# Both output projections of a two-layer hybrid decoder by seven products over pairs of token tiles

## What is computed

```python
def _cross_attn(x, mem_k, mem_v, wq, wo):
    q = (x @ wq).reshape(B, T, XA_HEADS, XA_HEAD_DIM)
    s = jnp.einsum('bthd,bnhd->bhtn', q, mem_k).astype(F32) * XA_HEAD_DIM ** -0.5
    p = jax.nn.softmax(s, axis=-1).astype(x.dtype)
    o = jnp.einsum('bhtn,bnhd->bthd', p, mem_v).reshape(B, T, -1)
    return o @ wo

def _layer(x, pos, mem_k, mem_v, state, P):
    ...
    mix = jnp.concatenate([y_m, y_r, y_g, y_w], axis=-1).astype(x.dtype) @ P['w_out']
    x = _layer_norm(ALPHA * x + mix, P['ln1_g'], P['ln1_b'])
    x = _layer_norm(ALPHA * x + _cross_attn(x, mem_k, mem_v, P['xa_wq'], P['xa_wo']), P['ln2_g'], P['ln2_b'])
    ff = jnp.square(jax.nn.relu(x @ P['w_up'])) @ P['w_down']
    x = _layer_norm(ALPHA * x + ff, P['ln3_g'], P['ln3_b'])
```

## Time and profile before

| | |
|---|---|
| Time, median of 3 runs (range) | 2280.8 us (2274.9 to 2288.0) |
| Profiled execution, span from first to last instruction | 2275.9 us |
| PE busy | 2222.5 us, 98% |
| DVE busy | 1096.5 us, 48% |
| ACT busy | 431.2 us, 19% |
| POOL busy | 115.4 us, 5% |
| Granted TensorE clock, mean | 0.994 |

### The profile page before, as it was taken

The page is one execution under the profiler, slowest core; times in us unless marked ns, Lnnn a source line. Parts: engine busy times, 40 slices in busy tenths (PEclk is TensorE's granted clock), DMA queues, the critical chain, the costliest instruction groups (busy, mean ns, idle before and its releaser), DMA issues. The chain is left out here.

```text
span 2275.9 us, 32156 instructions
## 1 busy us (share of the span) xinstructions
PE 2222.5 (98%) x13494; PEld 1626.9 (71%) x13494; DVE 1096.5 (48%) x1951; ACT 431.2 (19%) x915; POOL 115.4 (5%) x208
## 2 busy tenths in 40 slices
PE   7999999999999999999999999999999999999997
PEld 5877765547855888888888777565488468888885
DVE  5652246545425444765166422655354364447643
ACT  2332122021311222000023321311114012120000
POOL 0111101000100000000002111010000000000000
PEclk9999999999999999999999999998999999999998
DMA  7121114234442122222142112233346222222221
GB/s 282 55 72 40 50 47 122 86 105 185 185 148 93 53 96 74 74 74 90 58 132 75 38 40 58 55 109 109 114 151 223 107 93 74 74 94 92 75 74 39
DMA packets 136335, 217.27 MB, mean 95 GB/s; under 512 B 33672, under 2 KB 67776, under 8 KB 136064
## 3 DMA queue, kind: packets, MB, share of 16 engines
q1 hardware_dynamic: 133888, 211.02, 27.1%
q10 hardware_dynamic: 2304, 4.20, 0.5%
HBM read 198.39 MB, written 14.58 MB: 94 GB/s over the span
## 5 line engine op out<-in xcount | busy, mean ns | idle before, releaser
L727 PE MATMUL psum<-xT,ring 128*128 128x256 f32 (+1 forms) x768 | 222.1, 415 | 0.1
L2270 PE MATMUL psum<-tmp 128*128 128x272 f32 x768 | 181.4, 393 | 0.1
L2270 PEld LDWEIGHTS psum<-tmp 128*128 128x128 f32 x768 | 145.8, 190 | 30.8 <-issue 0.9
L727 PEld LDWEIGHTS psum<-xT,ring 128*128 128x128 f32 x768 | 131.3, 189 | 35.2 <-issue 10.2
L724 PE MATMUL psum<-ring,ext 128*128 128x512 f32 x256 | 126.0, 629 | 0.0
L677 PE MATMUL psum<-xT,ring 128*128 128x256 f32 (+1 forms) x512 | 120.3, 394 | 4.4 <-ACT big L1817 2.0
L2371 PE MATMUL psum<-big,ring 128*128 128x256 f32 (+1 forms) x512 | 118.4, 393 | 0.0
L677 PEld LDWEIGHTS psum<-xT,ring 128*128 128x128 f32 x512 | 96.3, 190 | 25.7 <-issue 4.6
L2689 PE MATMUL psum<-ring,big 128*128 128x512 f32 x256 | 113.1, 595 | 0.0
L827 PE MATMUL psum<-ring,big 128*128 128x512 f32 x256 | 111.9, 594 | 0.0
L2371 PEld LDWEIGHTS psum<-big,ring 128*128 128x128 f32 x512 | 97.0, 190 | 19.8
(11 more groups left out here) (494 smaller groups left out, 3553.8 us busy)
## 6 DMA issues: line engine op xcount, KB each, us to landing
ring<-in_w_down SPq DMA_DIRECT2D x16, 2048.0 KB, 7.7
ring<-in_w_in SPq DMA_DIRECT2D x14, 2048.0 KB, 8.6
ring<-in_w_up SPq DMA_DIRECT2D x14, 2048.0 KB, 7.7
big<-in_cache_mem_k SPq DMA_DIRECT2D x16, 1024.0 KB, 6.9
ring<-in_xa_wk SPq DMA_DIRECT2D x4, 2048.0 KB, 8.7
ring<-in_xa_wv SPq DMA_DIRECT2D x4, 2048.0 KB, 10.3
ring<-in_w_out SPq DMA_DIRECT2D x4, 2048.0 KB, 9.1
ring<-in_xa_wq SPq DMA_DIRECT2D x4, 2048.0 KB, 7.9
```

Of the source, the lines that this page charges most:

```text
L727: ins = pe.matmul(bank[:, :c.stop - c.start], wring[:, n % 2, k, i * P:(i + 1) * P], xTv[:, k, c], start=(k == 0), stop=(k == KC - 1))
L2270: ins = pe.matmul(ps[:, :HT], left[:, k, :], right[:, k, :], start=(k == 0), stop=(k == KH - 1))
```

## The change

Each of the two output projections is computed for pairs of token tiles, (0, 1) and (2, 3). With input halves by depth (first and last four chunks of 128) and output halves of 512 columns, a pair takes seven products of four chunks (numbered 1 to 7) where it took eight. Products 1, 2, 4 and 5 start a bank; 6 is piled on 1's bank, 3 on 5's, 7 on 6's, each after DVE has read what is there. The sums of weights are made on POOL, the sums of inputs on DVE. `residual` is called 18 times in a projection where it was called 10 times; eight of the 18 are a plain addition. Transposed x has its columns in a new order (`PLACE`): tiles 0, 1, the samples, 2, 3, in the layers' two normed x that feed the query and the MLP.

```diff
+PLACE = [0, P, 2 * P + NS, 3 * P + NS, 2 * P]
+TOKEN_PAIRS = ((0, 1), (2, 3))
...
+            def pair_product(pe, pre, p, i, bank, left, right):
+
+                ps = bk.begin(pe, (pre, p, i), bank)
+                for k in range(4):
+                    ins = pe.matmul(ps, left(k), right[:, k, :], start=(k == 0 and i in (1, 2, 4, 5)), stop=(k == 3), skip_group_check=True)
+                bk.filled(ins, (pre, p, i))
...
             def wout_ahead(pe):
 
-                for half in range(2):
-                    slab_wait(pe, 11 + half)
+                slab_wait(pe, 11)
                 pe.wait_ge(sig["yC"], sig.at("yC", 1))
                 pe.wait_ge(sig["yD"], sig.at("yD", 1))
-                for T in range(2):
-                    wout_tile(pe, T, range(4, KC))
+                for p in range(2):
+                    wout_product(pe, p, 2, p)
+                pe.wait_ge(sig["wright"], sig.at("wright", 3))
+                for p in range(2):
+                    wout_product(pe, p, 4, 2 + p)
+
+            def wout_weights(g):
+
+                bk.take(g, ("Bsc", 4))
+                slab_wait(g, 11)
+                slab_wait(g, 12)
+                w0, w1 = wring[:, 1], wring[:, 0]
+                t1, t2, t4 = wout_right
+                after(g, g.tensor_tensor(t1, w1[:, 0:4], w0[:, 0:4], ALU.subtract), "wright")
+                after(g, g.tensor_tensor(t2, w1[:, 4:8], t1, ALU.subtract), "wright")
+                after(g, g.tensor_tensor(t4, w0[:, 4:8], t2, ALU.subtract), "wright")
...
+                    wout_sums(v)
                     ps = bk.take(v, ("orow2",))
...
-                    turn_x_tensor(pe, bk, sig, LN1, 3, 4, (4, 5))
+                    turn_x_tensor(pe, bk, sig, LN1, 2, 3, (4, 5))
                     for u in range(4):
                         if u == 0:
                             q_first(2)
-                            for T in (4, 3):
+                            turn_x_tensor(pe, bk, sig, LN1, 3, 4, (4, 5))
+                            for T in (2, 3):
...
+                    def left_sums(p, which):
+
+                        ta, tb = (slice(TILES[T][0], TILES[T][0] + P) for T in TOKEN_PAIRS[p])
+                        for hp in range(2):
+                            bk.given(v, ("pv", TOKEN_PAIRS[p][1], hp))
+                        for j in which:
+                            if j in (1, 2):
+                                v.wait_ge(sig["aleft"], sig.at("aleft", 4 * p + j))
+                            a, b_, op = ((aT[:, 0:4, tb], aT[:, 4:8, tb], ALU.add), (left_a[0], aT[:, 0:4, ta], ALU.subtract),
+                                         (aT[:, 4:8, ta], left_a[1], ALU.subtract), (aT[:, 0:4, ta], aT[:, 0:4, tb], ALU.subtract))[j]
+                            sig.up(v.tensor_tensor(left_a[j], a, b_, op), "aleft")
...
                         if T < 3:
                             maxima(T + 1)
+                        if T == 2:
+                            left_sums(0, range(4))
...
                     for hp in range(2):
                         bk.take(g, ("s", 3, hp))
                     after(g, g.memset(pOwn, 0.0), "pOwn0")
+                    slab_wait(g, 15)
+                    slab_wait(g, 16)
+                    w0, w1 = wring[:, 1], wring[:, 0]
+                    after(g, g.tensor_tensor(right_a[0], w1[:, 0:4], w0[:, 0:4], ALU.subtract), "aright")
+                    after(g, g.tensor_tensor(right_a[1], w1[:, 4:8], right_a[0], ALU.subtract), "aright")
+                    bk.take(g, ("ss",))
+                    after(g, g.tensor_tensor(right_a[2], w0[:, 4:8], right_a[1], ALU.subtract), "aright")
```

More of the change, by code:

```diff
@@ new lines, in wout_last_weights, with wout_sums @@
+            def wout_last_weights(g):
+                bk.take(g, ("wout", "part", 1))
+                w1 = wring[:, 0]
+                after(g, g.tensor_tensor(w1[:, 0:4], w1[:, 4:8], w1[:, 0:4], ALU.subtract), "wright")
+            def wout_sums(v):
+                for n in "ABCD":
+                    v.wait_ge(sig["y" + n], sig.at("y" + n, 1))
+                tiles = [[slice(TILES[T][0], TILES[T][0] + P) for T in pair] for pair in TOKEN_PAIRS]
+                for p in range(2):
+                    tb = tiles[p][1]
+                    ins = v.tensor_tensor(quartered(wout_left[p][0]), y_low[:, :, :, tb], y_high[:, :, :, tb], ALU.add)
+                    sig.up(ins, "wleft")
+                for p in range(2):
+                    ta, tb = tiles[p]
+                    s1, s2, s4, s3 = (quartered(s_) for s_ in wout_left[p])
+                    if p == 0:
+                        v.wait_ge(sig["wleft"], sig.at("wleft", 2))
+                    sig.up(v.tensor_tensor(s2, s1, y_low[:, :, :, ta], ALU.subtract), "wleft")
+                    sig.up(v.tensor_tensor(s3, y_low[:, :, :, ta], y_low[:, :, :, tb], ALU.subtract), "wleft")
+                    v.wait_ge(sig["wleft"], sig.at("wleft", 3 * p + 3))
+                    sig.up(v.tensor_tensor(s4, y_high[:, :, :, ta], s2, ALU.subtract), "wleft")
@@ L834, in wout_ahead, with sample_fold, wout_tensor @@
+            def sample_fold(pe, pre, banks):
+                for half in range(2):
+                    bk.given(pe, (pre, "part", half))
+                    ps = bk.begin(pe, (pre, 4, half), banks[half])
+                    bk.filled(pe.matmul(ps[:NS, :], const("fold"), partial[:, half, :], start=True, stop=True), (pre, 4, half))
+            def wout_tensor(pe):
                 for half in range(2):
                     slab_wait(pe, 11 + half)
-                pe.wait_ge(sig["yC"], sig.at("yC", 1))
@@ L2224, in residual @@
                 ps = bk.take(v, key)
-                bk.give(v.scalar_tensor_tensor(x, x, ALPHA, ps[:n, :], ALU.mult, ALU.add), key)
-                bk.given(v, key)
+                if more:
+                    ins = v.tensor_tensor(x, x, ps[:n, :], ALU.add)
+                else:
+                    ins = v.scalar_tensor_tensor(x, x, ALPHA, ps[:n, :], ALU.mult, ALU.add)
+                if done:
+                    bk.give(ins, key)
+                    bk.given(v, key)
+                else:
+                    v.wait_ge(sig["v"], sig.up(ins, "v"))
             hT = cols(big, 0, FC, NT)
```

273 lines of the change are left out of this document (160 added, 113 removed).

## The result

The change makes the kernel slower: 2301.6 us median (2299.5 to 2306.9) against 2280.5 in the same runs, a ratio of 1.0104 with a 95% interval of 1.0077 to 1.0132. (The ratio is the record's estimate over the runs of both kernels; the two medians alone lie 21.1 us apart, 1.0093, inside the interval.) I had forecast 2290, within 0.5% of before, and a range of 2272 to 2302, whose upper end the time just meets. The profiled execution spans 2298.8 us, 22.9 more than before's.

A forecast was written before the change was run, and what follows sets the result against it. PE, busy 2222.5 of 2275.9 us, was taken to bound the kernel. Terms of +1.7 a layer, +3.4 in two, gave a 2279.3 span; 4.9 to the median made 2284.2, and the clock's 6.0 made 2290, range 2272 to 2302.

The forecast's parts named there:

- Saved products: Both output projections: 112 records of 128 by 512 instead of 128, -7.0 us each, -28.0 for four.
- The block's end: End of the first block: POOL's three weight sums and DVE's work alternate, next block starts later, +4.7 us a layer.
- The attention: Key copies in the attention: DVE's new sums wait for POOL's two, PE stops at the fourth group, +5.6 us a layer.
- The query and the MLP: Tile 3 turned behind the third first product, only transposes before product 2: PE idle, +3.85 us at each, per layer.
- The wait for tile 1's norm: Second projection: PE's 2.32 us idle for this norm goes, other products lie there, -2.3 us a layer.
- The clock: PE's clock falls in two of five idle stretches a layer, 1.5 us each, +6.0 us in all.
- The first rival: Clock falls at every pause over 3 us, four a layer, 1.4 to 1.75 us each: 2298; chance 0.25.
- The case of 2300: Rival: piled products wait for DVE's reads, one extra 2 us wait per projection, then the clock: 2300; chance 0.06.
- Transfers at nothing: Both projections: slabs and cached values are asked for no later relative to use, so transfers cost nothing.
- POOL's price: POOL's two-input weight sums, at the block's end and in the attention, taken at 3.7 us each.
- the 4.9 us that I took between span and median: The profiled execution's span lies 4.9 us below the median; left as is, taking 2279.3 to 2284.2.
- the blocking: Block's end and attention: DVE sums of two SBUF tiles do not run beside POOL's operations, so laid end to end.

The follow-up runs named there:

- e6_before_turns: The kernel before with only tile 3's turning moved behind the third first product, in query projection and MLP; ratio 1.0109.
- e3_pool_late: The changed kernel with POOL's first two weight sums of the second projection moved behind the last sample scores; ratio 1.0005 against the kernel before.
- e7_pieces: The changed kernel with POOL's first two weight sums of the second projection each cut into four of 128x512; ratio 1.0063 against the kernel before.
- e5_all: The changed kernel with turning order undone, POOL's two sums later, first projection's sums and products 4 in the next block; 2245.0 us, ratio 0.9843 against before.
- e4_next_block: The changed kernel with the first projection's weight sums, input sums and products 4 moved behind the barrier into the next block; ratio 1.0040 against before.
- e9_dve_sums: The e5_all kernel with seven of a layer's eight weight sums moved from POOL to DVE; ratio 0.9867 against the kernel before.

## Why the prediction was wrong

- **Saved products, -7.0 a projection:** right, to 0.1 us, in both kernels. That the piled products never wait was right too.
- **The block's end, +4.7:** the mechanism was right, the alternation of POOL and DVE row by row, and a term was mis-sized: POOL's sum, 4.5 for 3.7. Three of them are 2.4 us more, which gives 7.1; measured 6.6.
- **The attention, +5.6:** the same. Two sums of 4.5 give 7.2; measured 7.03.
- **The query and the MLP, +3.85 each:** right, PE is idle 3.69 each time; e6_before_turns has it alone.
- **The wait for tile 1's norm, -2.3:** right; the stage came to -5.47 for -5.45.
- **The clock, +6.0:** wrong in the count and in the price. I let it fall in two of five pauses a layer, for 1.5 us each, and no row said two. It fell behind each of the four over 3 us, of which the one ahead of products 4 is hidden behind DVE. The other three cost 5.7 us in layer 0 and 7.0 in layer 1, 12.6 for 6.0, that is 2.1 each. I also had the two pauses at the block's end the wrong way round: 2.3 ahead of products 4 and 4.3 ahead of the next block, where 4.49 and 2.27 were measured. The first rival, the clock at every long pause, is the mechanism that came true (2298, chance 0.25). The case of 2300 is nearer in number, but its mechanism, waits inside the piled products, did not occur.
- **Transfers at nothing:** right, no wait for one is new.

Put together: the waits and savings come to +4.8 us in layer 0 and +5.2 in layer 1 (0.3 of it a short wait for keys that I had not foreseen) where the forecast had +1.7, 6.6 in all, nearly all of it POOL's price; the clock behind the pauses is 6.6 more than forecast. 2290 + 6.6 + 6.6 is 2303, measured 2301.6. Either alone would have left the forecast 6 to 7 us short. That the sum comes so near is in part luck: the start of the program, +3.35, and the fall in layer 1's first block, 3.6 less than before, nearly cancel in the profile, and of the 4.9 us that I took between span and median 2.8 stand here.

Two steps failed, then: POOL's price of 3.7 us, where 4.5 was measured, and the clock's two falls a layer at 1.5 us, where three counted, at 2.1. The first goes back to the choice of the row. The earlier trace rows has the nearest number of columns, 2044, but its two sources are one array read at neighbouring columns. Before's trace also had POOL's 128x256 operation with two separate sources, 48 times at 0.72 us, which by the column is far above; even allowing for what a short operation costs at any size, I should have weighed it and did not. The page of the Trainium skill that I weighed and set aside, "GPSIMD Engine Reference", was right. Its factor of about 2 holds by DVE's own sum of 2048 columns: 4.50 to 2.29. I had made 5.4 of the factor by taking four sums of 512 columns, 0.68 each, for one of 2048. And its section "3.1 Elementwise — side-by-side cycle accounting" gives the pair for just this size, 4497 and 2293 ns, which the runs meet.

Of the blocking the Trainium skill, page "SBUF — State Buffer", section "🔬 SBUF: two separate sides", says that a VectorE operation with two inputs in SBUF and a GpSimd one that reads SBUF exclude each other for the length of the whole instruction. The rows of e3_pool_late and e7_pieces agree: 0.69 us away from POOL's sums against 4.25 and 4.87 beside them, and the second shows the instruction to be the unit: cut in four, POOL's sum adds 1.0 us to a sum of DVE's instead of 4.2.

## What to carry to other kernels

Before weight or input sums go on POOL, look what DVE has to do in that stretch: in this kernel each POOL sum stopped DVE's next sum of SBUF tiles until it had ended, so such sums belong where PE has work in hand and DVE has none that is due. Take an operation's price from a row with the same kinds of sources, not only the same size. And count a pause of PE like these, 3.0 to 7.0 us, at its length plus 1.4 to 3.1 us of slow products, at every place in every layer, unless it is hidden behind something else: of all such pauses in these profiles only one, in e6_before_turns, had fast products behind it. An order that keeps matmuls between a transpose and its first reader is worth more than it looks.

## What the runs showed of the hardware

- **A pause is charged by more than its length, and its length does not decide it.** At a block's start no slow products followed the pauses of 2.1 to 2.55 us; those of 3.01 and 3.10 were followed by 5.34 us for 3.64. In between it went both ways: 2.72 and 2.73 us were followed by 3.64 in layer 0 of e5_all and e4_next_block, but 2.72 in layer 1 of e9_dve_sums (and 2.83 in its layer 0) by slow products:

```profile
1587.53 5.34 PE L917 MATMUL psum<-ring,big 128*32 128x512 f32 x32 [2.72 <-PEq L943]
```

  In the attention a pause of 2.58 us was enough. In e6_before_turns one of 2.32 us was, and one of 3.69 was not.
- **The clock also falls where PE hardly pauses, or not at all.** Ahead of the first projection in layer 1, the profile of the kernel before has a stretch that I had passed over:

```profile
1550.00:1580.00 30.00, 28.95 (x210) 0.77 0.28 94
```

  That is 6.9 us lost, in a stage of many small products. The profile of the change has 0.89 over 1560 to 1590; that of e3_pool_late shows no fall there, but one at 340 to 350 (0.83) and one at 1460 to 1475 (0.89); that of e6_before_turns 0.50 from 1570 to 1590. The longest in e9_dve_sums, in the first block of layer 0, cost 10 us with PE busy all the time (stretch, its length, PE's busy time and records, granted clock, DMA share, GB/s):

```profile
435.00:455.00 20.00, 20.00 (x132) 0.50 0.00 1
```

  So such falls come in every profile here, the kernel before's too, at changing places and lengths. They are behind much of the scatter between single executions: with a mean granted clock of 0.996 e9_dve_sums took 2242 to 2245 us, with 0.988 to 0.991 it took 2252 to 2258; the kernel before, in the same runs, 2272 to 2277 with 0.995 to 0.997 and 2283 to 2285 with 0.991. What brings them on was not tried.
- **POOL's two-input operation came at two prices, at some 2000 columns:** 1.76 ns a column with both sources side by side in one slab, 2.2 with sources in two slabs or, for L875, 2048 columns apart in one (4.50 us). Why was not tried.
- **Not every DVE operation waits for POOL's sums.** Sums of two SBUF tiles did (4.25 to 4.99 us for 0.69). Those with a source in PSUM ran beside it at their own time (0.67 for 128x512). A scaling of 128x256 with its one source in SBUF waited, 3.32 us for 0.35, so it is not the two sources alone; but a reciprocal of one column, also from SBUF to SBUF, did not (0.16 us at 647.10 in e3_pool_late, beside POOL's sum, and 0.16 before).
